# Pairing the high and low activations of a k tile in one 512-wide product, in the 256-token upward projections

## The reference

```
def squared_relu_mlp(h, w1, w2):                  # first block, D_FF = 4096
    return jnp.square(jax.nn.relu(h @ w1)) @ w2
...
for l in range(DEPTH):                            # second block, D_FF_2 = 2816
    ...                                           # attention, x = x + mix @ w_out[l]
    h2 = rms_norm_2(x, ffn_norm_g[l])
    x = x + (jax.nn.silu(h2 @ w_gate[l]) * (h2 @ w_up[l])) @ w_down[l]
```

## Time and profile before

| | |
|---|---|
| median of 3 runs | 1610.06 us (1609.9 to 1611.47) |
| profiled execution, its own time | 1615.57 us |
| its span, first to last instruction | 1613.8 us |
| PE busy | 1563.6 us (97%), 9164 products |
| DVE busy | 1029.7 us (64%) |
| ACT busy | 795.2 us (49%) |
| mean granted clock of PE | 0.993 |

### The profile page before, as it was taken

One profiled execution on the slowest core, in us unless ns is written; L12 is line 12 of the kernel. 1 busy time (PEld: TensorE's weight loads), 2 busy tenths in 40 slices (PEclk: granted clock), 3 DMA queues, 4 the chain that ended last, 5 costly groups with the idle time before them and its releaser, 6 DMA issues.

```text
span 1613.8 us, 23480 instructions
## 1 busy us (share of the span) xinstructions
PE 1563.6 (97%) x9164; PEld 1283.3 (80%) x9164; DVE 1029.7 (64%) x1577; ACT 795.2 (49%) x1356; POOL 113.7 (7%) x130
## 2 busy tenths in 40 slices
PE   6999999999999999998999999999999999999999
PEld 2864788778888887577998777779998787699987
DVE  3637665455466447565875567868885658778863
ACT  3536634433255225654764456554544466554542
POOL 0111000000000001001000030100000111000000
PEclk8999999999999999999999999999999999999999
DMA  9438523577478424676987698336665695356653
GB/s 347 158 106 306 203 91 111 171 249 248 143 260 268 127 80 131 219 250 226 339 305 253 209 310 280 118 111 184 185 185 186 206 324 188 95 154 183 184 186 114
DMA packets 201005, 322.41 MB, mean 200 GB/s; under 512 B 14576, under 2 KB 100864, under 8 KB 200768
## 3 DMA queue, kind: packets, MB, share of 16 engines
q1 hardware_dynamic: 192992, 293.51, 56.9%
q0 software_dynamic: 7680, 27.34, 4.7%
q10 hardware_dynamic: 224, 0.07, 0.0%
HBM read 298.27 MB, written 22.61 MB: 199 GB/s over the span
## 4 chain that ended last, share of the span: by engine, by line
PE 89%; DVE 4%; ACT 2%; DMA 2%; issue 1%; POOL 0%; SPq 0%; POOLq 0%; DVEq 0%; ACTq 0%
PE bank L2195 55%; PE pair_bank L2195 22%; PE bank L2264 3%; PE pair_bank L2481 1%; PE bank L2512 1%; PE bank L2492 1%; DMA raw<-in_w_in 1%; PE pair_bank L2532 1%; PE bank L2792 1%; DVE w_lo L1556 1%; DMA raw<-in_w_ada 1%; PE bank L2290 1%; PE bank L2400 1%; PE bank L2546 1%; PE pair_bank L2535 0%
## 5 line engine op out<-in xcount | busy, mean ns | idle before, releaser
L1556 DVE TENSOR_TENSOR w_lo<-raw,w_hi 128x1024 fp32r<-128x1024 f32 (+2 forms) x374 | 447.9, 1219 | 272.2 <-ACT w_hi L1150 270.5
L1150 ACT CAST w_hi<-raw 128x1024 fp32r<-128x1024 f32 (+1 forms) x416 | 427.8, 1044 | 366.0 <-PE bank L2195 248.5
L2195 PE MATMUL pair_bank<-act_hi,w_hi 128*128 128x256 f32 (+1 forms) x744 | 229.5, 308 | 5.2 <-DVE act_lo L1669 3.1
L2195 PE MATMUL pair_bank<-act_hi,w_lo 128*128 128x256 f32 (+1 forms) x744 | 227.2, 305 | 0.0
L2195 PE MATMUL pair_bank<-act_lo,w_hi 128*128 128x256 f32 (+1 forms) x744 | 227.1, 305 | 0.0
L2195 PE MATMUL bank<-w_hi,hid_hi 128*128 128x512 f32 x560 | 221.8, 396 | 0.0
L2195 PE MATMUL bank<-w_hi,hid_lo 128*128 128x512 f32 x560 | 221.3, 395 | 0.0
L2195 PE MATMUL bank<-w_lo,hid_hi 128*128 128x512 f32 x560 | 221.3, 395 | 0.0
L2195 PE MATMUL bank<-w_hi,act_hi 128*128 128x512 f32 (+2 forms) x528 | 206.5, 391 | 8.2 <-DVE w_lo L1556 3.9
L2195 PE MATMUL bank<-w_hi,act_lo 128*128 128x512 f32 (+2 forms) x528 | 200.0, 379 | 0.0
L2195 PE MATMUL bank<-w_lo,act_hi 128*128 128x512 f32 (+2 forms) x528 | 199.7, 378 | 0.0
(11 more groups left out here) (249 smaller groups left out, 2104.6 us busy)
## 6 DMA issues: line engine op xcount, KB each, us to landing
raw<-in_w_mlp SPq DMA_DIRECT2D x128, 512.0 KB, 4.6
raw<-in_w_in SPq DMA_DIRECT2D x112, 512.0 KB, 4.5
raw<-in_w_ada SPq DMA_DIRECT2D x96, 512.0 KB, 5.7
raw<-in_w_gate SPq DMA_DIRECT2D x44, 512.0 KB, 3.8
raw<-in_w_up SPq DMA_DIRECT2D x44, 512.0 KB, 3.8
raw<-in_w_down SPq DMA_DIRECT2D x44, 512.0 KB, 3.6
split_lo<-w_lo POOLq DMA_DIRECT2D x36, 512.0 KB, 4.5
w_lo<-split_lo SPq DMA_DIRECT2D x36, 512.0 KB, 5.3
```

What stands on the lines that cost most here:

```text
L1150: nc.scalar.copy(hi_of(i)[:, 0:w], raw[:, i % RAW, 0:w]).then_inc(hi_ready, 1)
L1556: nc.vector.tensor_tensor(w_lo[:, i % RAW, 0:w], raw[:, i % RAW, 0:w], hi_of(i)[:, 0:w].bitcast(F32), ALU.subtract).then_inc(lo_ready, 1)
L2195: ins = nc.tensor.matmul(o, a[x], b[y], start=first and i == 0, stop=True, skip_group_check=True)
```

## The change

The high and low activations now lie in one tensor `act`. For the norms that feed the three 256-token stages (`BESIDE`), the low part of a k tile is written into the 256 columns beside its high part, where the context would stand. `beside` takes the place of `three`: one product of the high weights with both (512 columns: high x high into columns 0 to 255 of a bank, high x low into columns 256 to 511), then the low weights with the high activations (256 columns, onto columns 256 to 511). So a group f fills a whole bank, and its value is the sum of the bank's two halves. ACT copies the upper half to SBUF, and DVE adds the lower half to it.

In `up1` of layer 1 the groups take the banks 0, 1, 2 and 6 in turn. PE opens group 2j + f when DVE has made the sum of the group four before. DVE makes relu and square in one instruction, ACT casts it, DVE subtracts. In `up2` the gate and the upward projection take two banks each. The gate goes by tanh: silu(g) = g (tanh(g / 2) + 1) / 2; exp, add and reciprocal are gone. The eight banks are named as four pairs, and two transposed tiles of the norm ahead move to other banks.

```diff
-        act_hi = sb("act_hi", [P, KT, 2 * NT], F32R)
-        act_lo = sb("act_lo", [P, KT, 2 * NT], F32R)
+        act = sb("act", [P, 2, KT, 2 * NT], F32R)
+        act_hi, act_lo = act[:, 0], act[:, 1]
+        act_both = act_hi.rearrange("p k (i c) -> p k i c", i=2)
...
+        def up2_banks(j, which):
+
+            return pairs[((0, 3), (1, 2))[j % 2][which]]
...
         def up1_bank(l, h, idx):
 
+            if l:
+                return bank[(0, 1, 2, 6)[idx % 4]]
...
+                def drain_sides(j):
+                    if j >= 2:
+                        e.wait_ge(hidden, n.at("hidden", (l, h, j - 2)))
+                    for f in range(2):
+                        self.full(("up1", l, h, 2 * j + f))
+                        nc.scalar.copy(fa1[:, j % 2, f * NT:(f + 1) * NT], up1_bank(l, h, 2 * j + f)[:, NT:2 * NT]).then_inc(low_out, 1)
+                        n.put("low_out", (l, h, 2 * j + f))
+                    e.wait_ge(hidden_wide, n.at("hidden_wide", (l, h, j)))
+                    nc.scalar.copy(hid1_hi[:, j * 512:(j + 1) * 512], fa1[:, j % 2, :]).then_inc(squared, 1)
+                    n.put("squared", (l, h, j))
...
-                            self.order(nc.scalar.activation(fa2[:, j % 2, :], gb[:], ACT.Exp, scale=-1.0))
-                            nc.scalar.add(fa2[:, j % 2, :], fa2[:, j % 2, :], 1.0).then_inc(gate_exp, 1)
...
+                            nc.scalar.copy(tiles(fa2[:, j % 2, :], 2), up2_banks(j, 0)[:, :, NT:2 * NT]).then_inc(low_out, 1)
+                            n.put("low_out", ("gate", l, j))
+                            e.wait_ge(summed, n.at("summed", ("gate", l, j)))
+                            nc.scalar.activation(fb2[:, j % 2, :], fa2[:, j % 2, :], ACT.Tanh, scale=0.5).then_inc(gate_tanh, 1)
...
+                def sides(j):
+                    for f in range(2):
+                        t = fa1[:, j % 2, f * NT:(f + 1) * NT]
+                        e.wait_ge(low_out, n.at("low_out", (l, h, 2 * j + f)))
+                        nc.vector.tensor_tensor(t, up1_bank(l, h, 2 * j + f)[:, 0:NT], t, ALU.add).then_inc(summed, 1)
+                        n.put("summed", (l, h, 2 * j + f))
+                    e.wait_ge(summed, n.now["summed"])
+                    t = fa1[:, j % 2, :]
+                    nc.vector.scalar_tensor_tensor(t, t, 0.0, t, ALU.max, ALU.mult).then_inc(hidden_wide, 1)
+                    n.put("hidden_wide", (l, h, j))
+                    e.wait_ge(squared, n.at("squared", (l, h, j)))
+                    nc.vector.tensor_tensor(hid1_lo[:, j * 512:(j + 1) * 512], t, hid1_hi[:, j * 512:(j + 1) * 512].bitcast(F32),
+                                            ALU.subtract).then_inc(hidden, 1)
...
+            def beside(self, o, hi, lo, k, first):
+                nc.tensor.matmul(tiles(o, 2), hi, act_both[:, k], start=first, stop=True, skip_group_check=True)
+                return nc.tensor.matmul(o[:, NT:2 * NT], lo, act_both[:, k, 0], start=False, stop=True, skip_group_check=True)
...
+                            if q == 0 and idx >= 3 + l:
+                                if l:
+                                    e.wait_ge(summed, n.at("summed", (l, h, idx - 4)))
```

More of the change, by code:

```diff
@@ L209, in build @@
                 xn2 = sb("xn2", [P, TT, D], F32, s2)
-        pair_bank = top.enter_context(nc.psum_tensor("pair_bank", [P, 2, 512], F32))
-        bank = [pair_bank[:, i, :] for i in range(2)]
-        bank += [top.enter_context(nc.psum_tensor(f"bank{i}", [P, 512], F32)) for i in range(2, 8)]
+        pairs = [top.enter_context(nc.psum_tensor(f"pair_bank{i}", [P, 2, 512], F32)) for i in range(4)]
+        pair_bank = pairs[0]
+        bank = [p[:, i, :] for p in pairs for i in range(2)]
         split_lo = nc.dram_tensor("split_lo", (len(EARLY), P, 1024), F32).ap()
@@ L1468, in up1 @@
                         self.extras("mlp1", l, 32 * h + 2 * j + q)
-                    for f in (2 * j, 2 * j + 1) if l == 0 else (j,):
-                        drain(f)
+                    if l:
+                        drain_sides(j)
+                    else:
+                        drain(2 * j)
+                        drain(2 * j + 1)
             def rows2(self, l):
@@ L1718, in norm_low @@
                 self.e.wait_ge(norm_hi, n.at("norm_hi", (m, t, a)))
[L1719 to L1721 removed]
+                hi, lo = (normed(m, i, slice(4 * a, 4 * a + 4), NT + t * P, NT + (t + 1) * P) for i in range(2))
+                nc.vector.tensor_tensor(lo, tiles(turned_bank(m, t, a)[:], 4), hi.bitcast(F32), ALU.subtract).then_inc(norm_lo, 1)
                 n.put("norm_lo", (m, t, a))
@@ L2101, in up1 @@
                         self.extras("mlp1", l, 32 * h + 2 * j + q)
-                    for f in (2 * j, 2 * j + 1) if l == 0 else (j,):
-                        low(f)
+                    if l:
+                        sides(j)
+                    else:
+                        low(2 * j)
+                        low(2 * j + 1)
             def rows2(self, l):
@@ L2722, in up1 @@
                                     e.wait_ge(norm_lo, n.at("norm_lo", (m, X, k)))
-                                ins = self.three(o, [v[:, kk, f * P:(f + 1) * P] for v in w], [a[:, k, c0:2 * NT] for a in (act_hi, act_lo)],
-                                                 k == 0 and (l == 0 or f == 0))
-                            if l == 0 and q == 1 and f == 0:
+                                hi, lo = (v[:, kk, f * P:(f + 1) * P] for v in w)
+                                if l:
+                                    ins = self.beside(o, hi, lo, k, k == 0)
+                                else:
+                                    ins = self.three(o, (hi, lo), [a[:, k, :] for a in (act_hi, act_lo)], k == 0)
+                            if q == 1 and f == 0:
                                 self.filled(ins, ("up1", l, h, idx))
@@ L2801, in up2 @@
                     for which in range(2):
-                        b = bank[((0, 1), (2, 7))[j % 2][which]]
+                        b = up2_banks(j, which)
                         if j >= 2:
-                            if which == 0:
-                                e.wait_ge(drained_g, n.at("drained_g", (l, j - 2, 0)))
-                            else:
-                                e.wait_ge(gated, n.at("gated", (l, j - 2)))
+                            e.wait_ge(summed, n.at("summed", (("gate", "up")[which], l, j - 2)))
                         for q in range(2):
@@ L2815, in up2 @@
                                     k = 4 * q + kk
-                                    ins = self.three(b[:, f * NT:(f + 1) * NT], [v[:, kk, f * P:(f + 1) * P] for v in w],
-                                                     [a[:, k, NT:2 * NT] for a in (act_hi, act_lo)], k == 0 and f == 0)
+                                    ins = self.beside(b[:, f, :], *(v[:, kk, f * P:(f + 1) * P] for v in w), k, k == 0)
                             self.took(ins, ("up2", l, j, which) if q == 1 else None)
```

66 lines of the change are left out of this document (42 added, 24 removed).

## The result

| | median | runs | ratio to before, 95% interval |
|---|---|---|---|
| before | 1613.93 us (1609.9 to 1616.0) | 22 | |
| after | 1616.38 us (1612.28 to 1620.46) | 22 | 1.0019 [1.0012, 1.0025] |

The change makes the kernel 0.19% slower, some 3.1 us. The prediction had 2.6 us the other way and a range that ended at 1613. Its two terms have the right signs, but both are mis-sized in the same direction. The two profiled executions lie the other way round (1615.57 us before, 1614.55 after): each is one draw from runs that spread over 6 and 8 us.

A forecast was written before the change was run, and what follows sets the result against it. PE was taken as the bound, busy for 97% of the span. -8.8 us in both `up2` and +6.2 us from layer 1's `up1` gave -2.6 us, so 1607.5 us, with a range from 1598 to 1613.

The forecast's parts named there:

- The number 1607.5: Whole kernel: the forecast median in us after the change, 2.6 us or 0.16% less than before.
- The term of `up1`, +6.2: Layer 1's `up1` and the `down` behind it: 4.1 us later at the stage's end, 2.1 more in `down`.
- DVE's exchange: `up1` of layer 1: DVE's round trip to ACT becomes the bound, three pairs 18.8 us against PE's 16.6.
- 6.63 and 5.49 us: `up1` of layer 1: time between ends of relu-square, with three splits and with two, when neither waits for PE.
- I put the second cast at 764.5: `up1` of layer 1: second weight cast behind the ada slots at 764.5, relu-square of pair 3 ending at 768.3.
- The 2.1 us in `down`: `down` behind layer 1's `up1`: slots 33 and 35 start late behind DVE's last two pairs, adding 2.1 us.
- The term of `up2`, -8.8: Both `up2`: 704 groups on PE each save 12.5 ns, 8.8 us together.
- one of 512 and one of 256 (226.7 + 119.6 = 346.3 ns): `up2` on PE: price of a group after the change, against 358.8 ns for three products 256 wide.
- The second rival: Both `up2`: the joined product saves less, at 233.3 ns 4.1 us, giving 1612.2 us; chance 0.11.
- cover, put at 2.7 us in each j: `up2`: the loop through ACT and DVE takes 8.4 of 11.1 us, so it was costed at nothing.
- DVE keeping up (0.30): First rival, `up1` of layer 1: PE sets the pace throughout, -12.1 us, 1598.0 us; chance 0.30.
- an `up2` held by DVE and ACT (0.07): Third rival, `up2`: splits queue behind an exchange; at 11.8 us a j, 1622.9 us; chance 0.07.

The follow-up runs named there:

- e1: Only both `up2` changed against the kernel before, layer 1's `up1` left as before: 1609.19 us, ratio 0.9972.
- e10: e3's kernel with the joined product in both `up2` taken apart into three products 256 wide: 1612.06 us, ratio 0.9997 to the kernel before.
- e3: The whole change, with ACT's hidden cast and DVE's subtraction in layer 1's `up1` issued a pair later: 1608.51 us, ratio 0.9963 to the kernel before.
- e11: The same code as e3, run once more: 1606.52 us, ratio 0.9955 to the kernel before.
- e2: Only layer 1's `up1` paired against the kernel before, both `up2` with exp and reciprocal as before: 1620.87 us, ratio 1.0048.
- e8: The whole change, with only DVE's subtraction in layer 1's `up1` a pair later, ACT's order untouched: 1623.58 us, ratio 1.0073 to the kernel before.
- e9: e3's kernel with both products of a group 512 wide in both `up2`, which is more work: 1683.02 us, measured once.
- e7: The kernel before with only the gate changed to tanh, without exp, add and reciprocal: 1612.54 us, ratio 0.9995.
- e4: The whole change with five banks in turn instead of four in layer 1's `up1`: 1615.35 us, ratio 1.0020 to the kernel before.
- e6: e3's kernel with `up2`'s gate made by exp, add, reciprocal and a product again: 1620.96 us, ratio 1.0048 to the kernel before.
- e5: e3's kernel with four 512-wide then four 256-wide products, in both `up2` and most of layer 1's `up1`: 1607.63 us, ratio 0.9971 to the kernel before.

## Why the prediction was wrong

Its direction came from a sum of two terms, -8.8 and +6.2. The trace has -6.7 and +7.7, +1.0 together; the parts timed alone gave -4.5 (from -6.5 to -2.7 by the interval) and +7.7, and the whole +3.1 (1.9 to 4.0). Where the 2 us between the traces and the timed runs lie is open: e1's own trace has 122.3 and 124.0 us for the two `up2`, 6.5 saved, and its timed runs show 4.5. e10 against e3 and e11 gives 5.5 and 6.8. The number 1607.5 had a further fault that is not of the mechanism: it started from 1610.06, the median of three runs, and the median of 22 is 1613.93.

**The term of `up1`, +6.2: the mechanism is right, the size 1.5 us short.** It named DVE's exchange, and e2, e3 and e8 show it. The step times were right to a tenth: from the end of one relu-square to the next I had 6.63 and 5.49 us; the chain has 790.72 to 796.12 (5.40) with two splits, and 6.5 with three. The step that failed is the start: "I put the second cast at 764.5 ... and the end of relu-square of pair 3 at 768.3". I let an earlier PE bring the slots behind ada earlier. ACT in order of time in the changed kernel, against the earlier trace rows:

```profile
765.08 1.04 ACT L1170 CAST w_hi<-raw 128x1024 fp32r<-128x1024 f32 x1 [5.42 <-DMA raw<-in_w_mlp]
766.57 1.04 ACT L1170 CAST w_hi<-raw 128x1024 fp32r<-128x1024 f32 x1 [0.45 <-DMA raw<-in_w_mlp]
```

The first cast came 1.7 us later than before, not earlier, since its slot landed later, and PE waited 2.56 us for the split behind it. Relu-square of pair 3 ended at 770.27, 2.0 us after my 768.3. The ten pairs behind took 62.7 us (63.5 predicted), and `down` began at 839.09 instead of 837.5. The 2.1 us in `down` were 1.6.

**The term of `up2`, -8.8: mis-sized, the larger error (2.1 us by the traces, 4.3 by the timed runs).** The step that failed is "one of 512 and one of 256 (226.7 + 119.6 = 346.3 ns)": prices from runs of one width, added for products that alternate. In layer 0 this nearly held: 122.3 us are 347.4 ns a group, 0.3 from the sum of e9 and e10. In layer 1 it did not: 351.7 ns, of 12.5 ns only 7.4 saved. So 8.8 became 6.7. The second rival ("the joined product saves less") was in part true, through another mechanism than mine: not the dearer price of `down`, which e9 excludes. By the Trainium skill's rule in "TensorE: Matmul & The Clock Gate", section "Back-to-back issue gap", both `up2` would gain an estimated 1.8 us, and the total would be 1614.5 us (the prediction has 1614.6). The measured saving, 6.7 us by the traces and 4.5 by e1, is more than twice that.

**What was costed at nothing.** The tangent (e7), the banks (e4, e10) and the layout (e10) cost nothing. That `up2` costs nothing was right: PE never stops there. Its cover, put at 2.7 us in each j, was not measured; e6, which loads it with the reciprocal (3.36 us) and one more product (0.7), makes PE wait.

**The rivals.** DVE keeping up (0.30) was wrong for this order of instructions (e3 shows that DVE does keep up once the exchange is moved), and so was an `up2` held by DVE and ACT (0.07). I gave slower 0.15; the two terms could err in the same direction, and did.

**Open** is what sets 347.4 or 351.7 ns. It isn't the layer: e8 has 122.3 us in layer 1 too (1430.22 to 1552.52), and e4 has 123.8 in layer 0 (1088.51 to 1212.26). It isn't a wait: PE is busy throughout. Nor is it one price for a whole stage, as the starts of four slots of the changed kernel show, the third to the sixth of `up2` in layer 1 (a slot has eight groups):

```profile
1429.67 0.39 PE L2255 MATMUL pair_bank<-act,w_hi 128*128 128x512 f32 x1
...
1432.44 0.39 PE L2255 MATMUL pair_bank<-act,w_hi 128*128 128x512 f32 x1
...
1435.16 0.40 PE L2255 MATMUL pair_bank<-act,w_hi 128*128 128x512 f32 x1
...
1437.99 0.40 PE L2255 MATMUL pair_bank<-act,w_hi 128*128 128x512 f32 x1
```

The third slot takes 2.77 us, 346 ns a group, the fourth 2.72 (340), the fifth 2.83 (354). From the fifth slot on a group costs 351 to 355 ns, except in every sixth slot: the tenth has 350, the sixteenth 340, and so on in turn. In layer 0, at 122.3 us, a group costs 346 to 348 behind the first slot, and 350 in every sixth slot from the fifth. e1, e3, e4, e8 and e11 show these two patterns and no third; e3 has the dear one from the first slot of layer 1, e4 from the sixth slot of layer 0. Where the widths don't alternate, every sixth slot stands out too: 353 against 360 ns a group in e10 and in the kernel before, 460 against 453 in e9. Six is the number of `w_hi` buffers in the second block. That the price hangs on where the weights lie is a guess that no run tests, and what turns one pattern into the other stays open.

## What to carry to other kernels

When products get cheaper and the sums move to another engine, write down that engine's queue in order and look for a cross-engine round trip just ahead of the work that feeds TensorE. Issue the dependent cast and subtraction one unit later; here that turned 0.19% slower into 0.4% faster without taking away an instruction. And move both halves: moving the subtraction alone made it worse, since ACT's cast was what stood in the way. (Moving the cast alone was not run.)

An edit with no effect by itself (the tangent, 0.9995) can be what a second one needs (13.7 us). Test a part that frees an engine together with the part that loads it.

## What the runs showed of the hardware

**Alternating widths share their time out anew.** In the changed kernel's `up2` of layer 0, PE in time order:

```profile
1100.61 0.39 PE L2255 MATMUL pair_bank<-act,w_hi 128*128 128x512 f32 x1
1100.84 0.27 PE L2256 MATMUL pair_bank<-act,w_lo 128*128 128x256 f32 x1
1100.95 0.40 PE L2255 MATMUL pair_bank<-act,w_hi 128*128 128x512 f32 x1
```

From a 512-wide start to the next start there are 230 to 240 ns, and 110 to 120 behind a 256-wide one; alone they have 227.4 (e9) and 119.7 (e10). Only the sum of the two can be compared with the prices alone.

**A stage began 3 us later with a lower clock ahead of it.** The same 20 us, in e3's kernel and then in the change, with the granted clock third from the end of the line:

```profile
604.00:624.00 20.00, 17.21 (x90) 15.41 (x89) 13.95 (x23) 12.05 (x24) 0.54 (x1) 0.83 0.26 78
```

```profile
604.00:624.00 20.00, 17.86 (x95) 15.57 (x95) 14.94 (x24) 12.38 (x25) 0.54 (x1) 0.91 0.32 93
```

The code of this stretch is the same in both. 0.83 against 0.91 is some 3.2 us more at 1.2 GHz instead of 2.4. Counted from the first product of the first `down`, `up1` of layer 1 began 401.3 us later in e3 (334.16 to 735.50), but 398.6 in the change (333.42 to 732.00) and 398.4 in e11 (331.53 to 729.90), where this window has 0.91 too. All thirteen traces fall into these two groups: 398.2 to 398.8 us with 0.91 in this window (before, the change, e1, e6, e8, e11), 401.3 to 401.5 with 0.83 (e2, e3, e4, e5, e7, e9, e10). So the clock and the later start go together. That the clock is the cause is not shown, and 3.2 us at half the clock cost PE at most 1.6 us of work, so that this window alone doesn't account for the 3 us. It is why stages were compared from their own first product, and not by where they end in the span.
